# A three-block transformer kernel: mLSTM cells that keep scores and values for a chunk's second visit, with gate rows spread by DMA, and an output projection by seven products

## The chip, the cores and the metric

The kernel is one program on one core of a Trainium2 chip. The metric is the device time of one execution, in microseconds. All data are float32.

## What is computed

Three transformer blocks run one after the other on a sequence of 1024 tokens with 1024 channels. The change touches two places.

In the first block a bidirectional mLSTM runs over the sequence, with 4 heads (key width 64, value width 128), in chunks of 128 tokens, once forward and once backward over the same q, k and v, with gates of their own:

```python
def step(carry, blk):                      # one chunk of one direction
    C, n, m = carry
    b = jnp.cumsum(fb, axis=-1)
    D = jnp.where(lower, b[..., :, None] - b[..., None, :] + ib[..., None, :], -jnp.inf)
    m_t = jnp.maximum(b + m[..., None], D.max(-1))
    s = jnp.einsum('bhtd,bhsd->bhts', qb, kb) * jnp.exp(D - m_t[..., None])
    num = jnp.einsum('bhts,bhsv->bhtv', s, vb) + w_inter[..., None] * jnp.einsum('bhtd,bhdv->bhtv', qb, C)
    h = num / jnp.maximum(jnp.abs(den), jnp.exp(-m_t))[..., None]
    C_new = decay[..., None, None] * C + jnp.einsum('bhs,bhsd,bhsv->bhdv', wk, kb, vb)
```

Its normalised sum of both directions, beside a Fourier mixing of the other channels, is multiplied with `w_out` (named mix in the kernel), and `x = LN(ALPHA * x + (1 + g1) * mix)` follows. The second block holds latent attention (8 heads over 1024 tokens, causal) whose result is multiplied with a 1024 x 1024 matrix and added:

```python
o = causal_block_attention(q, k, v).reshape(B, S, ATTN_WIDTH)
x = x + (o * jax.nn.silu(gate)) @ w_out     # mla_out in the kernel
h = rmsnorm(x, conv_norm_g)
```

## The kernel before

The kernel is written in Bass: the program of each engine is written out by hand, and each cross-engine dependency is a wait on a semaphore. `steps(tag, names)` makes one semaphore with a list of names; `did(name)` raises it and `after(0, name)` is the wait for it. Each engine works strictly in the order in which its program is written. Activations lie with channels on the 128 partitions: X, H and the three parts A, B, C of one tensor ABC hold 8 tiles of 128x1024 each. Weights stream from HBM through a ring of 4 slots, in tiles of 128x1024, issued on SyncE's queue (SP). PSUM is one tensor, bank, of 8 banks of 128x512.

**The cells.** A cell is one chunk of one direction. There are 16; cell n is direction n % 2 and chunk n // 2 counted from that direction's start, so that cells 0 to 7 meet all eight chunks for the first time and cells 8 to 15 meet each for the second time. TensorE's order is front(n+1), back(n). Its front: four matmuls that copy a gate row of each head onto all 128 partitions by a selection matrix (L1187, into bank 0), two more for the weights of the queries (L1192, bank 1), four transposes of the values (L1197), four scores (L1203), two transposes of the keys (L1208). Its back: `out` of cell n, four matmuls with the weighted scores (L1220) and four with the running state (L1224), then `state` (L1231), whose result goes to bank 6. VectorE (DVE), for cell n+1: adds the causal mask to the copied rows (L1696, into weights_t), scales the queries (L1698), copies the values out of PSUM (L1703), multiplies scores and weights (`probs`, L1707); then for cell n: four operations on four columns, of which L1717 is the first and the reciprocal L1723 the last, and two that update the state (L1726). ScalarE (ACT), for cell n+1: four exponentials of the masked rows (`weights`, L1404), four scalings of the keys (L1408); then four that write out cell n (L1415) with the reciprocals. Behind cells 12, 14 and 15 DVE also takes statistics of finished chunks, whose two directions GpSimd (POOL) has added (L978). The first matmul behind the cells is L1253.

During the cells POOL multiplies the reloaded x by ALPHA (L980). The reload, one DMA of 4 MB (L964), is issued before the position transform that stands ahead of the cells. VectorE's first wait for it stands ahead of L313, the first of the small operations that prepare the fused layer norms.

**mla_out.** TensorE multiplies tile by tile (`linear`, L184): 8 output tiles by 2 halves of the tokens by 8 products of 128x128 by 128x512; each such product is two MATMUL instructions in the trace. VectorE adds each bank to X (L2485), ScalarE squares it and VectorE sums the squares for the norm that follows (L578). Other large projections of the kernel (`Seven`, `seven_products`, L718) already compute a pair of output tiles by seven block products in place of eight, from sums of the weights made by POOL (`seven_lhs`, L705 to L713, s1 to s4) and sums of the right-hand side (t1 to t4).

## Time and profile before

| | |
|---|---|
| median of 3 runs | 4214.31 us (4209.85 to 4216.12) |
| the profiled execution's own time | 4215.86 us |
| its span | 4214.1 us |
| TensorE busy | 4126.5 us, 98% of the span |
| VectorE, ScalarE, GpSimd busy | 1640.6, 823.3 and 787.9 us |
| the chain that ended last | TensorE 91%, VectorE 4%, ScalarE, issue, DMA and GpSimd 1% each |
| granted TensorE clock | 0.992 on the mean |

The span is the time from the first to the last instruction; the profiled execution's own time lies 1.8 us above it. A busy time counts an engine as busy while an instruction of its is in flight, whether the engine goes at its full rate or not.

### The profile page before, as it was taken

Reading aid. Unit: us, or ns where it says so; the run is one execution under the profiler, and the core shown is the slowest. Engines: PE = TensorE matmul, PEld = TensorE weight load, DVE = VectorE, ACT = ScalarE, POOL = GpSimd, SP = SyncE. Lnnn points to the kernel's source line nnn. Section 1 sums busy time; section 2 is a strip of 40 time slices with the busy share of each in tenths; the row PEclk is TensorE's granted clock in tenths of the full one; section 3 lists DMA queues with packets and bytes.
Section 4 is the critical chain, followed back from the end, with each engine's and each line's share of the span. In section 5 each row is a group of like instructions: output and inputs, shape, how many; then the busy total and the mean of one; then the engine's idle time right before and its main releaser. Section 6 shows DMA issues by size and latency. Waiting matters only on the chain.

```text
span 4214.1 us, 46243 instructions
## 1 busy us (share of the span) xinstructions
PE 4126.5 (98%) x19608; PEld 2128.0 (50%) x19608; DVE 1640.6 (39%) x2754; ACT 823.3 (20%) x1612; POOL 787.9 (19%) x511
## 2 busy tenths in 40 slices
PE   8999999999999999999999999999999999999999
PEld 3466444444444456664444444654599344444444
DVE  3656263333333323331799431535433322222311
ACT  3124110000002113221332311633243100000000
POOL 3320052324230200000363200000100032212210
PEclk9999999999999999999999999999999999999999
DMA  5420011111111120000111121001100121111121
GB/s 203 169 79 11 30 41 49 40 50 40 40 50 46 75 80 18 28 16 30 40 40 40 40 80 50 31 28 46 61 4 24 40 80 50 40 41 50 61 94 34
DMA packets 53629, 218.50 MB, mean 52 GB/s; under 512 B 6192, under 2 KB 7728, under 8 KB 51504
## 3 DMA queue, kind: packets, MB, share of 16 engines
q1 hardware_dynamic: 47520, 167.53, 11.5%
q0 software_dynamic: 5904, 48.01, 3.0%
q8 instruction: 156, 2.56, 0.2%
q14 instruction: 49, 0.40, 0.0%
HBM read 194.50 MB, written 18.89 MB: 51 GB/s over the span
## 4 chain that ended last, share of the span: by engine, by line
PE 91%; DVE 4%; ACT 1%; issue 1%; DMA 1%; POOL 1%; SPq 0%; DVEq 0%; POOLq 0%; ACTq 0%
PE bank L718 34%; PE bank L184 27%; PE bank L3227 4%; PE bank L3045 4%; PE bank L2054 2%; PE bank L3238 2%; PE bank L2143 1%; PE bank L2113 1%; PE bank L501 1%; PE bank L2929 1%; PE bank L2913 1%; PE bank L2097 1%; PE bank L2134 1%; PE bank L2944 1%; PE bank L3168 1%
## 5 line engine op out<-in xcount | busy, mean ns | idle before, releaser
L184 PE MATMUL bank<-H,ring 128*128 128x512 f32 x1792 | 778.1, 595 | 6.7 <-DVE ABC L3558 2.9
L184 PEld LDWEIGHTS bank<-H,ring 128*128 128x128 f32 x1792 | 339.5, 191 | 435.2 <-issue 430.6
L184 PE MATMUL bank<-ABC,ring 128*128 128x512 f32 x944 | 412.0, 594 | 1.1 <-DVE ABC L1836 0.7
L718 PE MATMUL bank<-H,ring 128*128 128x512 f32 x736 | 323.6, 592 | 1.0 <-ACT ABC L2221 0.8
L184 PEld LDWEIGHTS bank<-ABC,ring 128*128 128x128 f32 x944 | 177.2, 190 | 225.6 <-issue 222.8
L2522 DVE SCALAR_TENSOR_TENSOR bank<-ABC,params,bank 128x1024 f32<-128x1024 f32 x184 | 237.3, 1290 | 8.0
L718 PEld LDWEIGHTS bank<-H,ring 128*128 128x128 f32 x736 | 139.6, 190 | 178.0 <-issue 178.0
L718 PE MATMUL bank<-X 128*128 128x512 f32 x400 | 181.6, 597 | 3.1 <-POOL X L708 3.1
L3045 PE MATMUL bank<-H 64*64 64x64 f32 x5088 | 169.3, 220 | 10.7 <-DVE H L3662 6.0
L718 PE MATMUL bank<-H,X 128*128 128x512 f32 x400 | 179.8, 592 | 0.0
L3045 PEld LDWEIGHTS bank<-H 64*64 64x64 f32 x5088 | 160.0, 136 | 15.7 <-issue 6.5
L718 PE MATMUL bank<-X,ring 128*128 128x512 f32 x368 | 165.4, 592 | 0.0
L718 PE MATMUL bank<-ABC,ring 128*128 128x512 f32 x360 | 157.6, 592 | 0.0
L2000 POOL TENSOR_TENSOR ABC<-ABC 128x1024 f32<-128x1024 f32 x48 | 113.3, 2361 | 220.4 <-ACT ABC L2311 214.7
L1466 ACT ACTIVATE norm_room<-bank 128x512 f32<-128x512 f32 x30 | 17.9, 597 | 637.9 <-PE bank L718 637.9
L718 PEld LDWEIGHTS bank<-X 128*128 128x128 f32 x400 | 76.5, 191 | 100.0 <-issue 100.0
L718 PEld LDWEIGHTS bank<-H,X 128*128 128x128 f32 x400 | 76.0, 190 | 95.9 <-issue 95.2
L705 POOL TENSOR_TENSOR X<-ring 128x512 f32<-128x512 f32 x32 | 41.3, 1290 | 393.7 <-DMA ring<-in_gu 185.1
L718 PEld LDWEIGHTS bank<-X,ring 128*128 128x128 f32 x368 | 69.9, 190 | 88.0 <-issue 87.9
L718 PEld LDWEIGHTS bank<-ABC,ring 128*128 128x128 f32 x360 | 68.4, 190 | 86.1 <-issue 85.1
L718 PE MATMUL bank<-ABC,kept 128*128 128x512 f32 x256 | 111.2, 592 | 0.0
L1828 DVE SCALAR_TENSOR_TENSOR ABC<-bank,params,norm_room 128x512 f32<-128x512 f32 x60 | 45.0, 750 | 153.0 <-PE bank L718 153.0
(686 smaller groups left out, 5866.4 us busy)
## 6 DMA issues: line engine op xcount, KB each, us to landing
ABC<-in_ada SPq DMA_DIRECT2D x48, 512.0 KB, 5.1
ring<-in_gu SPq DMA_DIRECT2D x44, 512.0 KB, 4.4
ring<-in_up SPq DMA_DIRECT2D x32, 512.0 KB, 4.1
...
```

The lines of the kernel that those rows point to most:

```text
L184: mm = nc.tensor.matmul(bank[:, 2 * (m % 2) + h, :], ring[:, s % RING, k * P:(k + 1) * P], rhs(k)[:, h * HALF:(h + 1) * HALF], start=(k == ...
L501: mm = nc.tensor.matmul(bank[:, 2 * m + j, :], ring[:, s % RING, k * P:(k + 1) * P], half_of(H, k, j), start=(k == 0), stop=(k == DT - 1), ...
L718: mm = nc.tensor.matmul(S.bank(j, slot), lhs[:, k * P:(k + 1) * P], rhs[:, k, :], start=start and k == 0, stop=(k == 3), skip_group_check= ...
L1828: nc.vector.scalar_tensor_tensor(dst, product, par("b_ff1", 8 * g + tile_), base, ALU.add, ALU.add).then_inc(*S.did(f"c{c}", j))
L2000: nc.gpsimd.tensor_tensor(C[:, c, :], C[:, c, :], conv_parts[k % 2], ALU.add).then_inc(*conv_pool.did(f"tap{k}"))
L2054: mm = nc.tensor.matmul(bank[:, b + h, :], tile_of(hd, first + k), A[:, src + k, h * HALF:(h + 1) * HALF], start=(k == 0), stop=(k == n - 1))
L2097: return nc.tensor.matmul(score_bank(n)[:, a:z], own_half[side, LENGTHS[n] * P:(LENGTHS[n] + 1) * P], k_pe[side, a:z], start=False, stop=T ...
L2113: nc.tensor.matmul(score_bank(m)[:, a:z], q_n[:, b * P:(b + 1) * P], k_n[:, a:z], start=True, stop=False, skip_group_check=True)
L2522: nc.vector.scalar_tensor_tensor(conv_rows(c), conv_us[c % 4][:, k:k + SEQ], conv_tap(c, k), conv_rows(c), ALU.mult, ALU.add).then_inc(*co ...
L3045: mm = nc.tensor.matmul(bank[rows, b, q * width:(q + 1) * width], lhs(q)[rows], rhs(q)[rows], start=start and (q == 0 or stop), stop=stop, ...
L3227: mm = nc.tensor.matmul(bank[:, down_bank[b], :], lhs[:, k * P:(k + 1) * P], rhs[:, k, :], start=start and k == 0, stop=stop and k == 7, s ...
L3238: mm = nc.tensor.matmul(bank[:, down_bank[b], :], ring[:, down_tile(j, m, part) % RING, k * P:(k + 1) * P], half_of(ABC, 11 * part + k, h) ...
```

## The change

In the cells the copied rows come by DMA. SyncE writes the two kinds of gate rows to HBM (`rows_kept`) and reads them back for each cell, spread over the partitions, into three buffers in turn; the read for cell n waits for `out` of cell n-3. POOL adds the causal mask. Scores and values of a chunk are copied to X in its first visit and used again in its second. In the second visit the keys are scaled by one VectorE operation. The state product goes to banks 0 and 6 in turn, and the reciprocals have two buffers. The unscaled x is reloaded behind the cells, and ALPHA is put into the gain `mod[:, 16:24]` and into the layer norm's epsilon. In the second block, output tiles 0 to 5 of mla_out are made in three pairs by seven products each, and tiles 6 and 7 as before. Two of the seven products of the first pair stand in the last attention head's order. The sums of squares go by a room in SBUF.

```diff
-                dst = bank[:, N.banks[0] + h, :]
+                dst = bank[:, N.banks[0] + h, :] if N.room is None else N.room[:, h, :]
...
-            weights_t = [carve(512) for _ in range(2)]
+            weights_t = [carve(512) for _ in range(3)]
...
+            values = [by_head(X_flat[:, 516 * c:516 * c + 516]) for c in range(7)] + [carve(516, "p (h v) -> p h v", h=4)]
+            scores_kept = [X_flat[:, 4 * SEQ + 512 * c:4 * SEQ + 512 * c + 512] for c in range(NT)]
+            queries = [carve(256, "p (q t) -> p q t", q=2) for _ in range(3)]
...
# SyncE
+            stream(sp, "mix", 0, 2)
+            sp.wait_ge(*rows_dve.after(0, "r"))
+            sp.wait_ge(*rows_act.after(0, "r_wi"))
...
+            for n in range(CELLS):
+                i, d, c, now = cell_of(n)
+                if n == 3:
+                    stream(sp, "mix", 2, 4)
+                if n >= 3:
+                    sp.wait_ge(*cell_pe.after(0, f"out{n - 3}"))
+                sp.dma_start(weights_t[n % 3], rows_kept[0, d, c].rearrange("h t -> (h t)").partition_broadcast(P)
+                             ).then_inc(rows_spread[n % 3], 16)
+                for e in range(2):
+                    sp.dma_start(queries[n % 3][64 * e:64 * e + 64], rows_kept[1, d, c, 2 * e:2 * e + 2, :].partition_broadcast(64)
+                                 ).then_inc(rows_spread[n % 3], 16)
...
# GpSimd
-            pool.dma_start(X[:, :, :], io["x"]).then_inc(x_again, 16)
...
+            def masked(n):
+                i, d, c, now = cell_of(n)
+                pool.wait_ge(*spread_of(n))
+                rows = weights_t[n % 3].rearrange("p (h t) -> p h t", h=4)
+                nc.gpsimd.tensor_tensor(rows, rows, causal[:, d:d + 1, :].broadcast_to([P, 4, P]), ALU.add
+                                        ).then_inc(*cells_pool.did(f"masked{n}"))
...
-            for m in range(DT):
-                last = nc.gpsimd.tensor_scalar(X[:, m, :], X[:, m, :], ALPHA_1, None, ALU.mult)
+            for n in range(CELLS):
+                masked(n)
+                if n == 13:
+                    head_sums_of(5)
+            head_sums_of(6)
             pool.wait_ge(*cell_pe.all())
             pool.wait_ge(*cell_dve.all())
+            pool.dma_start(X[:, :, :], io["x"]).then_inc(x_again, 16)
...
# VectorE, for cell m = n + 1
-                    v.wait_ge(*cell_pe.after(0, f"bcast{m}"))
-                    nc.vector.tensor_tensor(weights_t[m % 2] ..., bank[:, 0, :] ..., causal ..., ALU.add)
+                    v.wait_ge(*spread_of(m))
+                    nc.vector.tensor_tensor(queries[m % 3], A[:, 0:2, now], queries[m % 3], ALU.mult
+                                            ).then_inc(*cell_dve.did(f"queries{m}"))
+                    if met_first(m):
+                        v.wait_ge(*cell_pe.after(0, f"values{m}"))
+                        nc.vector.tensor_copy(values[c][:, :, 0:P], by_head(bank[:, 7, :])).then_inc(*cell_dve.did(f"values{m}"))
+                        v.wait_ge(*cell_pe.after(0, f"scores{m}"))
+                        nc.vector.tensor_copy(by_side(scores_kept[c]), bank[:, 2:4, 0:256] ...).then_inc(*cell_dve.did(f"scored{m}"))
+                        v.wait_ge(*cell_dve.after(0, f"scored{m}"))
+                    else:
+                        v.wait_ge(*cell_pe.after(0, f"keys{m}"))
+                        nc.vector.tensor_tensor(keys_tok[m % 2], bank[:, 1, 256:512] ...,
+                                                token_cols[:, 1, c, 32 * d:32 * d + 4].unsqueeze(2).broadcast_to([P, 4, 64]), ALU.mult
+                                                ).then_inc(*cell_dve.did(f"keys{m}"))
+                    v.wait_ge(*cell_act.after(0, f"weights{m}"))
...
+                    nc.vector.tensor_tensor(probs_t[m % 2], scores_kept[c], weights_t[m % 3], ALU.mult).then_inc(*cell_dve.did(f"probs{m}"))
...
# second block, GpSimd: operands of mla_out's seven products
+            nc.gpsimd.tensor_tensor(t1_out, quarter(B, 0, 1), quarter(B, 0, 0), ALU.subtract).then_inc(*rhs_out.did("t1"))
+            seven_lhs(pool, S, 0, "s1", "s2", "s3", "s4")
+            pool.wait_ge(*mla_dve.after(0, "gated7_6"))
+            nc.gpsimd.tensor_tensor(t3_out[:, 0:3], quarter(B, 1, 1)[:, 0:3], quarter(B, 0, 1)[:, 0:3], ALU.subtract
...
+            pool.wait_ge(*mla_pe.after(0, "s7_7"))
...
# second block, TensorE
-            pe.wait_ge(*mla_dve.all())
-            pe.wait_ge(*taken("mla_heads"))
-            linear(pe, "mla_out", lambda k: B[:, k, :],
+            out_rest()
+            out_free = lambda i, slot: seven_out.after(i, {3: "w", 4: "t21", 7: "t22"}[slot])
+            for j in (1, 2):
+                seven_products(pe, seven_out, j, out_rhs, out_free)
+            pe.wait_ge(*seven_out.after(2, "v"))
+            linear(pe, "mla_out", lambda k: B[:, k, :], 6,
```

TensorE in the cells, before: one whole turn, the front of a cell and the back of the one ahead of it. The row numbers are lines of the kernel, and a matmul counts here as one row entry however many instructions the trace shows for it.

```order
L1187 MATMUL bank<-ABC,kept 128x128 x4
L1192 MATMUL bank<-ABC,kept 128x128 x2
L1197 MATMUL bank<-ident,ABC 128x128 x4
L1203 MATMUL bank<-ABC 128x128 x4
L1208 MATMUL bank<-ident,ABC 128x128 x2
L1220 MATMUL bank<-ABC,norm_room 128x129 x4
L1224 MATMUL bank<-ABC 128x129 x4
L1231 MATMUL bank<-ABC 64x129 x4
```

The change, the last turn whose front is a first visit and the first whose front is a second visit: L1236 are the values, L1242 the scores, L1248 the keys, L1260 and L1264 `out`, L1269 `state`.

```order
L1236 MATMUL bank<-ident,ABC 128x128 x4
L1242 MATMUL bank<-ABC 128x128 x4
L1248 MATMUL bank<-ident,ABC 128x128 x2
L1260 MATMUL bank<-X,norm_room 128x129 x4
L1264 MATMUL bank<-ABC 128x129 x4
L1269 MATMUL bank<-X,ABC 64x129 x4
L1248 MATMUL bank<-ident,ABC 128x128 x2
L1260 MATMUL bank<-X,norm_room 128x129 x4
L1264 MATMUL bank<-ABC 128x129 x4
L1269 MATMUL bank<-X,ABC 64x129 x4
```

The two selection lines are gone from every turn, and values and scores from the turns of the second visits.

GpSimd around the cells, before: the reload of x, the constants, the zeroing, the scaling of x, the six sums of finished chunks.

```order
L964 DMA X<-in_x 128x8192
L966 DMA kept<-in_lstm_const 128x1792
L971 MEMSET ABC 128x516 x2
L972 MEMSET ABC 128x516
L980 TENSOR_SCALAR X<-X 128x1024 x8
L978 TENSOR_TENSOR H<-H 128x512 x6
```

GpSimd at the same place in the change: L1019 is the mask, L1025 the sums.

```order
L1005 DMA kept<-in_lstm_const 128x768
L1010 MEMSET X 128x4 x7
L1010 MEMSET ABC 128x4
L1011 MEMSET ABC 128x516
L1019 TENSOR_TENSOR ABC<-ABC,kept 128x512 x14
L1025 TENSOR_TENSOR H<-H 128x512 x2
L1019 TENSOR_TENSOR ABC<-ABC,kept 128x512 x2
L1025 TENSOR_TENSOR H<-H 128x512 x2
L1033 DMA X<-in_x 128x8192
L1025 TENSOR_TENSOR H<-H 128x512 x2
```

The reload of x has moved from ahead of the cells to behind them, and sixteen mask operations stand where the scaling stood.

TensorE from the end of the last attention head through mla_out, in the change: L2210 is the head's output product, L2218 the transpose of it, L2226 the products of the first pair, L720 those of the other two pairs, L184 tiles 6 and 7.

```order
L2226 MATMUL bank<-ABC,ring 128x512 x2
L2218 MATMUL bank<-ident,H 128x128
L2226 MATMUL bank<-ABC 128x512 x2
L2218 MATMUL bank<-ident,H 128x128
L2226 MATMUL bank<-ABC 128x512 x2
L2226 MATMUL bank<-ABC,ring 128x512 x4
L2226 MATMUL bank<-ABC 128x512 x12
L720 MATMUL bank<-ABC,ring 128x512 x12
L720 MATMUL bank<-ABC 128x512 x16
L184 MATMUL bank<-ABC,ring 128x512 x20
L591 MATMUL bank<-mean_of,norm_room 128x1 x4
L184 MATMUL bank<-ABC,ring 128x512 x6
```

Before, one row stood between the last transposes (L2151) and the norm's sums (L589): 116 matmuls of L184, with 12 more behind. Now the pairs take 84 and tiles 6 and 7 take 32.

## Rows read from the trace of the kernel before

**Rows 1.** The page, first part: busy time, share, instructions of TensorE.

```profile
PE 4126.5 (98%) x19608; PEld 2128.0 (50%) x19608; DVE 1640.6 (39%) x2754; ACT 823.3 (20%) x1612; POOL 787.9 (19%) x511
```

**Rows 2.** Timeline of one turn: start, duration, engine, line, operation, [idle before <-releaser].

```profile
320.57 1.16 PE L1187 MATMUL bank<-ABC,kept 64*128 64x128 f32 x8
320.68 0.18 DVE L1723 RECIPROCAL small<-small 128x4 f32<-128x4 f32 x1
320.78 0.58 DVE L1726 SCALAR_TENSOR_TENSOR ABC<-ABC,small,bank 128x129 f32<-128x129 f32 x2
320.89 1.14 ACT L1415 ACTIVATE H<-bank,small 128x128 f32<-128x128 f32 x4 [1.14 <-DVE small L1723]
...
322.10 0.66 PE L1197 MATMUL bank<-ident,ABC 128*128 128x128 f32 x4
322.21 0.69 DVE L1696 TENSOR_TENSOR ABC<-bank,kept 128x512 f32<-128x512 f32 x1 [0.85 <-PE bank L1192]
...
322.82 0.41 DVE L1698 TENSOR_TENSOR ABC<-ABC,bank 128x256 f32<-128x256 f32 x1
322.94 1.28 ACT L1404 ACTIVATE ABC<-ABC,cols 128x128 f32<-128x128 f32 x4 [0.90 <-DVE ABC L1696]
323.14 0.68 DVE L1703 COPY ABC<-bank 128x512 f32<-128x512 f32 x1
...
323.33 0.44 PE L1208 MATMUL bank<-ident,ABC 128*128 128x128 f32 x2
...
323.61 1.06 PE L1220 MATMUL bank<-ABC,norm_room 128*128 128x129 f32 x8
324.12 0.89 ACT L1408 ACTIVATE ABC<-bank,cols 128x64 f32<-128x64 f32 x4
324.32 0.69 DVE L1707 TENSOR_TENSOR norm_room<-bank,ABC 128x512 f32<-128x512 f32 x1 [0.49 <-ACT ABC L1404]
...
325.24 0.66 PE L1231 MATMUL bank<-ABC 128*64 128x129 f32 x8
325.36 0.16 DVE L1717 TENSOR_SCALAR small<-bank 128x4 f32<-128x4 f32 x1 [0.35 <-PE bank L1224]
...
325.95 0.18 DVE L1723 RECIPROCAL small<-small 128x4 f32<-128x4 f32 x1
```

**Rows 3.** Timeline of TensorE: both ends of the cells, and two groups early in them.

```profile
286.55 1.13 PE L1187 MATMUL bank<-ABC,kept 64*128 64x128 f32 x8 [1.94 <-DVE ABC L1666]
...
290.94 2.07 PE L1187 MATMUL bank<-ABC,kept 64*128 64x128 f32 x8
...
296.47 1.87 PE L1220 MATMUL bank<-ABC,norm_room 128*128 128x129 f32 x8
...
378.63 7.13 PE L1253 MATMUL bank<-ABC,ring 128*128 128x512 f32 x16
```

**Rows 4.** Windows: stretch, length, busy by engine, then granted clock, DMA share, GB/s.

```profile
260.00:263.00 3.00, 3.00 (x19) 3.00 (x18) 0.00 (x0) 0.00 (x0) 0.00 (x0) 0.60 0.97 407
293.00:300.00 7.00, 7.00 (x47) 5.75 (x46) 3.25 (x10) 2.37 (x9) 0.00 (x0) 0.63 0.01 2
364.00:368.00 4.00, 2.51 (x24) 2.03 (x23) 3.38 (x17) 1.49 (x6) 0.00 (x0) 1.00 0.00 0
```

**Rows 5.** DMA issues by tile: queue, count, KB each, median us to landing.

```profile
H<-ABC POOLq DMA_DIRECT2D x8, 256.0 KB, 3.2
...
X<-in_x POOLq DMA_DIRECT2D x1, 4096.0 KB, 14.5
```

**Rows 6.** One line of POOL: duration ns min/median/max, first and last start.

```profile
L713 POOL TENSOR_TENSOR X<-ring,X x32: 1257/1272/2256, 78.7 to 3896.3; 128x512 f32<-128x512 f32 x32
```

**Rows 7.** Timeline: DVE's first instruction behind its wait for x.

```profile
407.66 0.16 DVE L313 COPY kept<-params 128x8 f32<-128x8 f32 x1
```

**Rows 8.** Timeline of TensorE: the last transpose of the last head, and mla_out.

```profile
1894.51 0.30 PE L2151 MATMUL bank<-ident,H 128*128 128x128 f32 x1 [0.47 <-DVE ABC L2455]
1895.19 99.83 PE L184 MATMUL bank<-ABC,ring 128*128 128x512 f32 x232 [0.38 <-DVE ABC L2455]
```

318 lines of the change are left out of this document (216 added, 102 removed).

## The prediction

> **What bounds the kernel now.** I read the page first: TensorE is busy for 98% of the span [rows 1], so a change gains what it takes out of TensorE's order, as long as no other engine becomes the bound where TensorE is relieved. The change sits in two stretches: the cells, from 286.55 us to 378.63 us [rows 3], 92.1 us for sixteen cells, and mla_out, which starts at 1895.19 us [rows 8]. For the cells I then read the timeline of one turn [rows 2]. The reader is to see two things in it. TensorE has no gap: L1187, L1197, L1208, L1220 and L1231 begin as the group ahead of them ends. And beside TensorE runs a ring of ACT and DVE that is nearly as long. From one reciprocal to the next it is 5.27 us (320.68 to 325.95): 0.21 until ACT starts to write the cell out (L1415, 1.14), 0.91 in which ACT waits for the masked rows, 1.38 from the start of the exponentials (L1404) to the start of `probs` (L1707), 0.69 of `probs`, 0.35 of waiting for TensorE's `out`, 0.59 from L1717 to the reciprocal. The sum is 5.27.
>
> **The cells, step by step.** TensorE loses the selections in every turn: 320.57 to 322.10, 1.53 us. In the second visits it also loses values and scores, 322.10 to 323.33, 1.23 us. Its turn is then 5.27 - 1.53 = 3.74 us, and 2.51 us in second visits.
>
> The ring decides in their place. POOL now masks far ahead of ACT, so the 0.91 goes; `out` of a cell no longer stands behind the selections, so the 0.35 goes. What is left is 0.21 + 1.14 + 1.38 + 0.69 + 0.59 = **4.01 us**, since the kernel still has ACT write out cell n before it exponentiates for cell n+2, and DVE do `probs` before the reciprocals. `probs` reads SBUF alone now; L1707 with one PSUM operand is the nearest row, and I keep its 0.69. I check the others against 4.01. DVE in a first visit: 0.41 + 0.68 (values) + 0.68 (scores out, taken as a copy like L1703) + 0.69 + 3 x 0.16 + 0.18 + 0.58 = 3.70; in a second visit the two copies go and a scaling of 256 columns comes, 0.41 like L1698: 2.75. ACT: 1.14 + 1.28 + 0.89 = 3.31, and 2.42. A second ring runs through TensorE, because banks 4 and 5 are single: ACT's end of `out` (0.21 + 1.14), then 1.63 of L1220 and L1224 (323.61 to 325.24), then 0.59, with two hand-overs of 0.1: 3.8. All lie under 4.01, but none far under it in the first visits. So moving the keys to DVE in the second visits gives nothing by itself: ACT had the time.
>
> The new feed. The read for cell n waits for `out` of cell n-3, which ends some 0.8 before that cell's reciprocal. The exponentials of cell n start 1.35 after the reciprocal of cell n-2, that is 4.01 + 1.35 = 5.36 after that of cell n-3. Between stand three DMAs (256 + 64 + 64 KB) and a mask. The trace has no such read. Its nearest row is H<-ABC, 256 KB in 3.2 us [rows 5]; by bytes, 384 KB are 4.8, and one after the other at most twice the row, 6.4. I take 4.0, near the single row, because the three are issued together. The mask is 1.27 by POOL's 128x512 rows, 2.26 at the longest [rows 6]. Ready at -0.8 + 4.0 + 1.27 = 4.5, with 0.9 to spare; with 4.8 nothing is lost; with 6.4 and 1.27 the period becomes 5.5, with 6.4 and 2.26 it becomes 6.5.
>
> By the Trainium skill's page GPSIMD Engine Reference (Specifications), GpSimd shares its SBUF interfaces with VectorE and contends with VectorE instructions that have two SBUF inputs; the queries and `probs` become such instructions here. By that rule each mask would cost the long value of [rows 6], still inside the 0.9 us within 0.1; an estimate from that page therefore moves the sum by under 2 us.
>
> How many turns gain. `out` of cells 0 to 14 is followed by a turn with a front. Two of these turns lie in the cold start, treated below; one (cell 12) also has statistics on DVE, which stay. That leaves 12 plain turns and the one with statistics, each shorter by 5.27 - 4.01 = 1.26: 13 x 1.26 = **16.4 us**. The tail (out14, out15, whose ACT wait remains) is unchanged.
>
> The cold start. TensorE had waited 1.94 before the first cell, and soon after it goes at the lower of its two levels, 1.2 of 2.4 GHz: L1187 takes 2.07 at 290.94 where it takes 1.16 later [rows 2, 3], and 293 to 300 has a mean of 0.63 [rows 4], which puts the rise at about 298. At 2.07 / 1.16 = 1.8 cell 1's selections take 2.7, those of cells 0 and 2 some 1.5 each, 6 us that fall away, but what moves up into their place then runs cold itself. I take 4; ends 2 and 6.
>
> Behind the cells. The reload now starts after the last state update, on the old time axis about a microsecond behind 378.63 [rows 3], and takes 14.5 [rows 5]; DVE first asks for x at 407.66 [rows 7]. The 28 us of head norms, gating and first products hide it with 13 to spare; without that cover it would cost up to 14.5. The scaling by ALPHA on POOL had been hidden too and gives nothing. SP's writes of the gate rows (ten small DMAs) stand ahead of the position transform, and the first three cells' reads beside it. The mix tiles 2 and 3 are queued behind the first three cells' reads, tiles 4 on behind the sixteenth's; the first is wanted only when tiles 0 and 1 are done, so both are covered.
>
> Cells: 16.4 + 4 = 20.4 us.
>
> **mla_out.** Three pairs save four 128x512 products each, 12 in all, 24 instructions. 232 instructions take 99.83 us [rows 8], 0.430 each: 24 x 0.430 = **10.3 us**. Two products move into the tail of the last head and fill its waits for DVE, 0.47 and 0.38 [rows 8]: 0.85. The new operands: POOL's three operations of 1536 columns, some 3.8 each by three times [rows 6], start during the last head, the second of them with the head's last scores, and the first product that needs them has three products of 4 x 2 x 0.430 = 3.4 in front of it, two in the head and one behind. DVE's load per pair is about thirteen 512-column operations of 0.69, 9 us in 24. Nothing of this is late. Sum 11.2 us.
>
> **Sum.** 20.4 + 11.2 = 31.6 us; I take off 1.3 for masks at the long value. 30.3 against the profiled execution's 4215.86 (span 4214.1 and 1.8 around it) is 4185.6; the runs' median is 1.55 lower, so **4184 us**.
>
> **Rivals.**
> *The clock falls in the second visits.* TensorE works there for 2.5 of 4.0 us. For it: the clock fell to 0.60 while TensorE looked fully busy with narrow matmuls in 260 to 263 us [rows 4], and it fell as the cells began. Against it: in 364 to 368, with 2.51 of 4.00 us busy, it stayed at 1.00. At the lower level L1220 takes 1.87 and not 1.06 [rows 3]; the ring through TensorE becomes 0.21 + 1.14 + 3.0 + 0.2 + 0.59 = 5.1. Eight such cells at 1.1 more: +9, **4193**; half of them, 4189. The Trainium skill's page TensorE: Matmul & The Clock Gate (A second HAM failure mode: psum-queue depth-cycling) states that small idle gaps between groups of matmuls, when banks are cycled, make the clock swing between its two levels; by that page this rival would happen.
>
> *The spread rows come late.* If the feed takes 4.8 with long masks or 5.5 or so, the period is 4.5 to 5.5: at 5.0, 13 x 1.0 = +13, **4197**. For it: the cells' own chain has 0.9 us of slack and nothing else. Against: the DMA engines' share in the cells is 0.00 to 0.01 [rows 4].
>
> *The seven products bring nothing*, because operands or the extra additions on DVE hold TensorE: +11, **4195**. Other projections of this kernel run so with TensorE at 98%.
>
> *Slower than before.* One mechanism: the feed's round trip becomes the period. It has to exceed 6.5 us per cell (13 x 2.5 = 32.5 us given back), that is, over 6.4 for the three DMAs with every mask at 2.26. At 7.5 us per cell the time is 4184 + 13 x 3.5 = **4230**. Nothing in the rows shows such a read in a quiet stretch.
>
> **How the numbers follow.** Forecast 0.64 (own range 4177 to 4190; 4177 if the cold start gives 6, the ring's hand-overs overlap by 0.1 to 0.2 per engine and masks are short), clock 0.13, late rows 0.13, no gain in mla_out 0.06, slower 0.02, not as any of these 0.02. The range 4176 to 4197 holds the first three and most of the fourth. What a measurement can tell from no change is about 0.2%, 8.4 us, so faster means under 4206: 0.95; same 0.02; slower 0.03.
>
> **What would show each step.** TensorE's `out` (L1260) should come every 4.0 us in the middle of the cells, with ACT back to back from L1415's successor to the exponentials, and idle time of TensorE waiting for ACT or DVE. POOL's mask should end before ACT asks. If ACT's exponentials wait for POOL and POOL for DMA, the late rows are right; if matmul durations double behind cell 8, the clock. The cells should take about 72 us, mla_out to its norm's last sum about 11 us less. The wait for x behind the cells should not appear. I would be wrong above all if a ring that I did not trace holds the first visits, where DVE, TensorE and the ring lie within 0.3 us of each other.

## The result, and the profile after

| | before | after |
|---|---|---|
| median | 4212.08 us (4207.58 to 4216.12, 4 runs) | 4185.34 us (4183.71 to 4190.48, 4 runs) |
| ratio, with its 95% interval | | 0.9939 [0.9922, 0.9956] |
| the profiled execution's own time, span | 4215.86, 4214.1 us | 4184.5, 4181.1 us |
| TensorE busy | 4126.5 us | 4080.3 us |
| granted TensorE clock, mean | 0.992 | 0.993 |

The change makes the kernel 26.7 us faster by the medians. The forecast was 4184 us, 30.3 us under the execution that was profiled before.

The page of the changed kernel, first part, answers to [rows 1]: TensorE has 312 instructions fewer and is busy for 46 us less.

```profile
PE 4080.3 (98%) x19296; PEld 2090.1 (50%) x19296; DVE 1657.8 (40%) x2767; ACT 817.1 (20%) x1583; POOL 817.8 (20%) x541
```

The total hides a miss. I followed the landmarks of TensorE from stretch to stretch:

| from, to | before | after | gain |
|---|---|---|---|
| start of the program, first matmul of the cells | 286.55 | 284.57 | 2.0 |
| the cells, to the first matmul behind them | 92.08 | 76.12 | 16.0 |
| the first matmul behind the cells, to the first of L184 | 36.14 | 36.59 | -0.4 |
| last query-key product of the last head, to the sums of mla_out's norm | 109.11 | 96.84 | 12.3 |
| the whole span | 4214.1 | 4181.1 | 33.0 |

The row behind the cells comes up again with e1. The rest, some 3.2 us, lies in code that the change doesn't touch. The 2.0 ahead of the cells is scatter too: with the new code the first matmul of the cells starts anywhere from 284.4 to 287.0 us in the runs below. The largest pieces are places where the clock was granted differently in the two executions. These windows show two of them (columns as in [rows 4]): before, and then after.

```profile
20.00:60.00 40.00, 36.63 (x191) 20.03 (x184) 22.93 (x46) 19.28 (x28) 0.00 (x0) 0.91 0.58 229
1418.00:1438.00 20.00, 20.00 (x72) 11.90 (x71) 0.81 (x5) 3.53 (x7) 4.98 (x4) 0.83 0.16 53
```

```profile
20.00:60.00 40.00, 36.63 (x196) 19.43 (x189) 22.86 (x46) 20.60 (x29) 0.52 (x1) 0.96 0.59 231
1400.00:1420.00 20.00, 20.00 (x87) 12.28 (x86) 2.42 (x7) 3.53 (x7) 4.96 (x4) 0.91 0.15 53
```

So the two stretches of the change are worth 16.0 + 12.3 = 28.3 us, against 20.4 + 11.2 forecast (31.6, less 1.3). The cells fell short by 4.4 and mla_out brought 1.1 more.

**Where the cells fell short.** I cut them in three by the starts of `out` (L1260): from the cells' first matmul to out of cell 1 it was 16.0 us before and 8.31 after; from out 1 to out 12, eleven turns, 57.90 and 50.00; from out 12 to the first matmul behind, 18.18 and 17.81. The middle piece should have shrunk to 11 x 4.01 = 44.1. This is one of its turns in the timeline of the changed kernel, a first visit (weight loads are left out); it answers to [rows 2].

```profile
308.27 0.69 DVE L1753 TENSOR_TENSOR norm_room<-X,ABC 128x512 f32<-128x512 f32 x1 [0.39 <-DVE X L1742]
308.38 1.70 POOL L1019 TENSOR_TENSOR ABC<-ABC,kept 128x512 f32<-128x512 f32 x1 [2.97 <-DMA ABC<-rows_kept]
...
308.94 0.33 SPq L974 DMA_DIRECT2D ABC<-rows_kept  x1
308.95 0.16 DVE L1763 TENSOR_SCALAR ABC<-bank 128x4 f32<-128x4 f32 x1
309.14 0.97 DVE L1765 TENSOR_TENSOR ABC<-ABC,cols 128x4 f32<-128x4 f32 x1
...
310.14 0.16 DVE L1767 TENSOR_TENSOR ABC<-bank,ABC 128x4 f32<-128x4 f32 x1
310.34 0.18 DVE L1769 RECIPROCAL ABC<-ABC 128x4 f32<-128x4 f32 x1
310.43 0.58 DVE L1772 SCALAR_TENSOR_TENSOR ABC<-ABC,small,bank 128x129 f32<-128x129 f32 x2
310.55 1.14 ACT L1455 ACTIVATE H<-bank,ABC 128x128 f32<-128x128 f32 x4 [1.55 <-DVE ABC L1769]
...
310.93 0.42 DVE L1736 TENSOR_TENSOR ABC<-ABC 128x256 f32<-128x256 f32 x1
...
311.79 1.13 PE L1260 MATMUL bank<-X,norm_room 128*128 128x129 f32 x8 [0.69 <-DVE ABC L1736]
```

Look at L1765. It works on 128x4 numbers, as L1767 does in 0.16 us, and takes 0.97. It starts 0.76 after POOL's mask (308.38) and ends with it (310.08, 310.11). The reciprocal, ACT's `out` and TensorE's next `out` stand behind it. Without the 0.81 the turn of 4.67 us would be 3.86.

The second visits of the same trace (TensorE and the operations beside the mask) show both what was forecast and a second loss.

```profile
321.12 1.13 PE L1260 MATMUL bank<-X,norm_room 128*128 128x129 f32 x8 [1.93 <-DVE ABC L1747]
322.17 1.27 POOL L1019 TENSOR_TENSOR ABC<-ABC,kept 128x512 f32<-128x512 f32 x1 [2.75 <-DMA ABC<-rows_kept]
...
322.21 1.78 DVE L1753 TENSOR_TENSOR norm_room<-X,ABC 128x512 f32<-128x512 f32 x1 [1.20 <-ACT ABC L1443]
...
325.94 2.06 PE L1260 MATMUL bank<-X,norm_room 128*128 128x129 f32 x8 [0.86 <-DVE ABC L1747]
...
331.25 1.13 PE L1260 MATMUL bank<-X,norm_room 128*128 128x129 f32 x8 [1.13 <-DVE ABC L1747]
...
335.11 1.13 PE L1260 MATMUL bank<-X,norm_room 128*128 128x129 f32 x8 [1.13 <-DVE ABC L1736]
```

At 322.21 `probs` (0.69) takes 1.78, again to the end of a mask. At 325.94 `out` takes 2.06 in place of 1.13: the clock has fallen. From 331.25 on the turn is 3.86 us. The windows of the changed kernel around the fall:

```profile
317.00:321.00 4.00, 2.19 (x24) 1.53 (x22) 3.51 (x10) 2.44 (x11) 1.64 (x1) 1.00 0.33 79
321.00:325.00 4.00, 3.88 (x26) 2.90 (x26) 2.70 (x8) 1.48 (x7) 1.27 (x1) 0.66 0.18 49
325.00:329.00 4.00, 3.14 (x17) 2.73 (x16) 1.52 (x4) 1.99 (x8) 1.27 (x1) 0.50 0.41 76
329.00:333.00 4.00, 2.87 (x30) 2.16 (x28) 2.49 (x9) 2.29 (x8) 0.00 (x0) 0.99 0.28 98
```

TensorE had been busy for 2.19 of 4 us before it fell to the lower level, while DVE was held.

**mla_out.** TensorE's timeline at the end of the last head in the changed kernel, which answers to [rows 8]: products of the first pair (L2226) stand where TensorE had waited for DVE, and no wait of TensorE for another engine is left.

```profile
1874.20 0.27 PE L2218 MATMUL bank<-ident,H 128*128 128x128 f32 x1
...
1875.20 1.88 PE L2226 MATMUL bank<-ABC,ring 128*128 128x512 f32 x4
1876.92 0.27 PE L2218 MATMUL bank<-ident,H 128*128 128x128 f32 x1
1877.03 1.88 PE L2226 MATMUL bank<-ABC 128*128 128x512 f32 x4
1878.75 0.27 PE L2218 MATMUL bank<-ident,H 128*128 128x128 f32 x1
1878.86 1.88 PE L2226 MATMUL bank<-ABC 128*128 128x512 f32 x4
1880.58 3.60 PE L2226 MATMUL bank<-ABC,ring 128*128 128x512 f32 x8
```

The wait for x behind the cells doesn't appear: DVE's L313 starts at 390.16, the reload was issued at 362.1 and took 12.4.

### The profile page after: what moved, and what is told of

Its sections match the earlier page's. It is cut to its first block, busy times and chain, and to the rows that moved or that the text cites. A ratio compares the mean times of both kernels' runs of the same rounds, so it can differ in the third digit from the quotient of the medians.

```text
span 4181.1 us, 45680 instructions
## 1 busy us (share of the span) xinstructions
PE 4080.3 (98%) x19296; PEld 2090.1 (50%) x19296; DVE 1657.8 (40%) x2767; ACT 817.1 (20%) x1583; POOL 817.8 (20%) x541
## 4 chain that ended last, share of the span: by engine, by line
PE 84%; DVE 5%; ACT 1%; issue 1%; DMA 1%; POOL 1%; SPq 0%; DVEq 0%; POOLq 0%; ACTq 0%
PE bank L720 32%; PE bank L184 25%; PE bank L3397 4%; PE bank L3215 4%; PE bank L2121 2%; PE bank L3408 2%; PE bank L2210 1%; PE bank L2180 1%; PE bank L501 1%; PE bank L2164 1%; PE bank L3099 1%; PE bank L3083 1%; PE bank L2201 1%; PE bank L3114 1%; PE bank L3338 1%
## 5 line engine op out<-in xcount | busy, mean ns | idle before, releaser
L184 PE MATMUL bank<-H,ring 128*128 128x512 f32 x1792 | 780.5, 596 | 6.2 <-DVE ABC L3728 2.9
L184 PEld LDWEIGHTS bank<-H,ring 128*128 128x128 f32 x1792 | 340.4, 191 | 436.3 <-issue 431.8
L184 PE MATMUL bank<-ABC,ring 128*128 128x512 f32 x752 | 329.5, 595 | 0.7 <-DVE ABC L1882 0.7
L720 PE MATMUL bank<-H,ring 128*128 128x512 f32 x736 | 323.6, 592 | 1.2 <-ACT ABC L2346 0.8
L184 PEld LDWEIGHTS bank<-ABC,ring 128*128 128x128 f32 x752 | 140.8, 190 | 179.6 <-issue 177.3
L720 PEld LDWEIGHTS bank<-H,ring 128*128 128x128 f32 x736 | 139.6, 190 | 178.2 <-issue 178.2
L720 PE MATMUL bank<-X 128*128 128x512 f32 x400 | 179.9, 592 | 3.1 <-POOL X L710 3.1
L720 PE MATMUL bank<-ABC,ring 128*128 128x512 f32 x416 | 182.1, 592 | 0.0
L720 PE MATMUL bank<-H,X 128*128 128x512 f32 x400 | 179.9, 592 | 1.2 <-POOL H L1051 1.2
L720 PE MATMUL bank<-X,ring 128*128 128x512 f32 x368 | 165.5, 592 | 0.0
L720 PEld LDWEIGHTS bank<-ABC,ring 128*128 128x128 f32 x416 | 79.0, 190 | 99.5 <-issue 98.5
L720 PEld LDWEIGHTS bank<-X 128*128 128x128 f32 x400 | 75.9, 190 | 99.1 <-issue 98.9
L720 PEld LDWEIGHTS bank<-H,X 128*128 128x128 f32 x400 | 75.9, 190 | 97.2 <-issue 94.7
L720 PEld LDWEIGHTS bank<-X,ring 128*128 128x128 f32 x368 | 69.8, 190 | 88.2 <-issue 88.2
L720 PE MATMUL bank<-ABC,kept 128*128 128x512 f32 x256 | 111.2, 592 | 0.0
```

Of the source, the lines that this page charges most:

```text
L184: mm = nc.tensor.matmul(bank[:, 2 * (m % 2) + h, :], ring[:, s % RING, k * P:(k + 1) * P], rhs(k)[:, h * HALF:(h + 1) * HALF], start=(k == ...
L720: mm = nc.tensor.matmul(S.bank(j, slot), lhs[:, k * P:(k + 1) * P], rhs[:, k, :], start=start and k == 0, stop=(k == 3), skip_group_check= ...
```

## The experiments

My theory, H: POOL's mask and a VectorE operation that reads two SBUF inputs keep each other waiting, and the feed's timing puts the mask onto L1765. The rivals: VectorE is simply full in the first visits, or L1765 is slow for another reason. All the stretches are in one table behind the experiments. The runs of one kernel lie 4 to 13 us apart, so the stretches carry the argument. A turn is the time from one `out` (L1260) to the next.

**e1 and e2: the two halves apart.** e1 has only the changes to the cells, e2 only those to mla_out. Seen from the changed kernel, e1 has mla_out as it was,

```diff
-            out_rest()
...
+            linear(pe, "mla_out", lambda k: B[:, k, :],
```

and e2, seen from the changed kernel, has among others

```diff
-                    v.wait_ge(*spread_of(m))
...
+                    v.wait_ge(*cell_pe.after(0, f"bcast{m}"))
```

> The kernel before with the change to the cells alone; mla_out is made as before. If the two parts add up, the cells bring here what the profile of the whole change shows for them: 92.1 us before, 76.1 after, from the first matmul of the cells to the first behind them, so 16 us, and the time is about 4212 - 16 = 4196. My blind sum had 19 to 20 for them (4192). Rival: the new cells also disturb or help something behind them (the reload of x, the mix tiles queued behind the reads); then the landmarks behind the cells stand more or less than 16 us earlier than before.

> The kernel before with mla_out by seven products alone. If the two parts add up: 12.3 us of gain, the time about 4200. My blind sum had 11.2. Rival: the sum of the two gains in e1 and e2 differs from the 27 to 28 us of the whole by more than 3 us, so one part helps the other.

e1: 4203.36 us (4196.95 to 4209.77, 10 runs), ratio 0.9981 [0.9972, 0.9991]. e2: 4202.78 (4198.27 to 4209.16, 10 runs), ratio 0.9975 [0.9966, 0.9984]. e2's stretch of mla_out takes 96.83 us, as in the whole change. e1's cells take 78.9 us, 2.8 more than the same code in the whole change, with first visits of 4.67 again. By their times the parts give 0.0044 of the time together and the whole gives 0.0061; with the intervals that is no difference I can tell, though e1 alone gives less by its time (3.8 to 11.8 us) than the 13.2 of its stretch.

The rival of e1 is partly true. From the first matmul behind the cells to the first of L184 it takes 38.2 us, 2.1 more than before, so that the gain of 13.2 has shrunk to 11.1 there: ACT lets TensorE wait 0.94 in place of 0.55, and the clock is at its lower level once more (0.50 over 374 to 377 us; 1.00 over 379 to 400 before), where sixteen of the products take 8.70 in place of 7.03. Seven executions have such a stretch, of 38.2 to 38.4 us (e1, e3, e5, e6, e7, e8, e10); the changed kernel, e4, e9, e11 and e12 have 36.5 to 36.6, and e2 with the old cells 36.2. What decides it wasn't tried.

So mla_out's part is sharp, and that of the cells is 13 to 16 us, depending on how often the mask meets DVE and on how long the clock is low behind cell 12 (0.50 over all of 350 to 363 in e1), less 0.4 to 2.1 behind them.

**e3: the mask made short.** One column of each head is masked, in the same place with the same waits; the exponentials are those of unmasked rows.

```diff
-                nc.gpsimd.tensor_tensor(rows, rows, causal[:, d:d + 1, :].broadcast_to([P, 4, P]), ALU.add
+                nc.gpsimd.tensor_tensor(rows[:, :, 0:1], rows[:, :, 0:1], causal[:, d:d + 1, 0:1].broadcast_to([P, 4, 1]), ALU.add
```

> The changed kernel with the causal mask added to one column of each head in place of 128, so that POOL's operation keeps its place and its waits but is short. The exponentials are then those of unmasked rows: part of the computation is left out. Theory H (a VectorE operation with two SBUF inputs and POOL's mask hold each other up): the 128x4 operation L1765 goes back from 0.97 us to 0.16 in the first visits, their period from 4.67 us to 3.86, and over six or seven turns the cells get 5 to 6 us shorter, 76.1 to about 70.5; time about 4180. Rival R1 (VectorE's own work, or the ring of ACT and DVE, holds the first visits at 4.67, and the long L1765 only fills a wait): the period stays at 4.6 to 4.7 and the cells at 76 us. Rival R2 (the long L1765 is something else, a late semaphore or the read by DMA in flight at that time): L1765 stays at 0.9 or more, since the reads stand as before.

4177.07 us (4172.29 to 4182.05, 4 runs), ratio 0.9921 [0.9906, 0.9936]. The timeline of a first visit in e3:

```profile
305.82 0.69 DVE L1753 TENSOR_TENSOR norm_room<-X,ABC 128x512 f32<-128x512 f32 x1 [0.39 <-DVE X L1742]
...
306.50 0.16 DVE L1763 TENSOR_SCALAR ABC<-bank 128x4 f32<-128x4 f32 x1
306.70 0.16 DVE L1765 TENSOR_TENSOR ABC<-ABC,cols 128x4 f32<-128x4 f32 x1
306.72 0.21 POOL L1019 TENSOR_TENSOR ABC<-ABC,kept 128x4 f32<-128x4 f32 x1 [3.65 <-DMA ABC<-rows_kept]
306.90 0.16 DVE L1767 TENSOR_TENSOR ABC<-bank,ABC 128x4 f32<-128x4 f32 x1
```

L1765 takes 0.16, the turns from out 1 to out 12 are 3.87 us each, first visits and second visits alike, and the cells take 68.9 us. From 289 to 345 us the clock stays at 1.00, though TensorE is busy for only 2.87 of 4 us in the second visits: the fall at 321 us came with the hold. H stands; that VectorE is full (R1) and that the reads slow it (R2) fall, since both are unchanged here.

**e4: the keys back on ACT.** The change's own edit, undone alone.

```diff
-                    if met_first(n + 1):
-                        act.wait_ge(*cell_pe.after(0, f"keys{n + 1}"))
+                    act.wait_ge(*cell_pe.after(0, f"keys{n + 1}"))
...
-                    else:
-                        v.wait_ge(*cell_pe.after(0, f"keys{m}"))
-                        nc.vector.tensor_tensor(keys_tok[m % 2], ...
```

> The changed kernel with the keys of the second visits scaled by ACT in four operations, as in the first visits and as before the change. Theory (the second visits run at the length of a ring, recip, ACT's out, exponentials, probs, and ACT had time for the keys): the period of the undisturbed second visits stays at 3.86 to 3.9, the cells at 76 us within 1, and the time is the same within what can be measured. Rival (VectorE's one operation relieves ACT, as the edit's form suggests): the period grows by up to ACT's 0.93 us, the cells by up to 8 x 0.9 = 7 us. Second rival (the one operation hurts VectorE and TensorE waits for it, as the releaser L1747 in the list of waits says): the period falls by 0.3 to 0.4, the cells by 2 to 3 us.

4186.74 us (4183.29 to 4191.24, 4 runs), ratio 0.9945 [0.993, 0.9959]: the same by its time. But the turns of the second visits were 4.56 to 5.31 us, and out 1 to out 12 took 52.8 us against 50.0 to 51.1 for the code of the change. This looked like the first rival. The timeline of e4 speaks for another reason:

```profile
334.79 0.16 DVE L1757 TENSOR_SCALAR ABC<-bank 128x4 f32<-128x4 f32 x1
334.94 1.26 POOL L1019 TENSOR_TENSOR ABC<-ABC,kept 128x512 f32<-128x512 f32 x1 [3.73 <-DMA ABC<-rows_kept]
334.99 1.24 DVE L1759 TENSOR_TENSOR ABC<-ABC,cols 128x4 f32<-128x4 f32 x1
```

The mask meets the 128x4 operation in the second visits too. Whether ACT's four operations cost anything besides had to be asked without the hold (e9).

**e5: the mask moved in time.** Nothing is left out; POOL waits for VectorE's queries, and a fourth buffer keeps the mask early enough for ACT.

```diff
-            weights_t = [carve(512) for _ in range(3)]
+            weights_t = [carve(512) for _ in range(4)]
...
                 pool.wait_ge(*spread_of(n))
+                if n:
+                    pool.wait_ge(*cell_dve.after(0, f"queries{n - 1}"))
```

> The changed kernel with four buffers for the spread rows in place of three, so that each read is issued one cell earlier, and POOL's mask for cell n waits also for VectorE's queries of cell n-1. Nothing is left out. The mask then starts behind the queries, while VectorE copies from PSUM, in place of beside L1765. Theory H (two engines on two SBUF inputs each hold each other up): L1765 takes 0.16 us in every cell, all plain turns come every 3.87 us as in e3, the cells take 69 to 71 us, the time is about 4178. In the second visits the mask can still touch the start of probs, for 0.1 us. Rival R2 (what e3 removed was the work of the mask as such, or the waits around it): the first visits stay at 4.6 or more. Rival R3 (the hold moves to another operation of VectorE): L1736 or L1753 grow by as much as L1765 shrinks.

4177.16 us (4172.65 to 4184.33, 4 runs), ratio 0.991 [0.9895, 0.9925]. A first visit of e5: the mask stands beside the copies from PSUM.

```profile
311.19 0.42 DVE L1738 TENSOR_TENSOR ABC<-ABC 128x256 f32<-128x256 f32 x1
311.53 0.68 DVE L1742 COPY X<-bank 128x512 f32<-128x512 f32 x1
...
311.75 1.27 POOL L1021 TENSOR_TENSOR ABC<-ABC,kept 128x512 f32<-128x512 f32 x1 [2.58 <-DVE ABC L1738]
...
312.13 0.68 DVE L1744 COPY X<-bank 128x512 f32<-128x512 f32 x1
```

All eleven turns are 3.87 us, 42.53 together, and the cells take 68.85 us. The full mask is made, so it isn't its work but its place that cost 7.3 us beside the changed kernel's 76.12, and 10 beside e1. The fourth buffer isn't what brings it: e3 has the same turns with three.

**e6: TensorE kept busy in the second visits.**

```diff
+                if not met_first(n):
+                    for h in range(4):
+                        nc.tensor.transpose(bank[:, 7, h * P:(h + 1) * P], A[:, 4 + h, now], ident[:, :])
```

> The changed kernel with four transposes per second visit put back in TensorE's order (the values of the chunk once more, into bank 7, read by nobody), 0.66 us each time. The clock had fallen to 0.66 and 0.59 at the first two second visits (321 to 330 us), behind a stretch in which TensorE was busy for 2.19 of 4 us. If the fall is from TensorE's idleness at that place, the two turns of 4.82 and 5.31 us become 3.9 to 4.7, the cells 2 to 3 us shorter. Rival (the fall comes from something else, or from the waits on VectorE, which stay): both turns stay, and the cells are as long as before or up to 0.66 longer per turn where TensorE is the bound. In e3, where the hold was gone, TensorE was busy for 2.87 of 4 us and the clock stayed at 1.00, which speaks for the first.

4190.88 us (4187.2 to 4193.73, 4 runs), ratio 0.994 [0.9923, 0.9956]. My expectation failed: the second visits took 4.83 to 5.07 us, out 1 to out 12 52.9, L1770 (L1765 of the change) had a median of 0.63 us over its 16 cells, and the clock fell to 0.68 at 329 to 333 all the same. The added transposes shifted the second visits so that the mask kept meeting VectorE. So it says nothing about the clock by itself, and no run here fills the place with matmuls other than transposes.

**e7: late rows, made to happen.** Two buffers in place of three.

```diff
-                if n >= 3:
-                    sp.wait_ge(*cell_pe.after(0, f"out{n - 3}"))
+                if n >= 2:
+                    sp.wait_ge(*cell_pe.after(0, f"out{n - 2}"))
```

> The changed kernel with two buffers for the spread rows in place of three: the read for cell n waits for out of cell n-2. This makes the rival of the prediction, late rows, happen. By the rows of the changed kernel the loop over two cells is: issue 0.1, landing 3.9, mask 1.27, exponentials to the start of probs 1.49, probs 0.69, out 0.1 + 1.79, together 9.3 us, 4.67 per cell. The first visits stay near 4.67 (if the mask still meets L1765 there they get longer, up to 5.1), the second visits grow from 3.87 to about 4.67, ACT's exponentials wait for POOL, and the cells take 79 to 84 us, the time 4188 to 4194. If the feed had more slack than I think (a read faster than 3.9 in this pattern), nothing changes.

4212.65 us (4208.61 to 4220.42, 10 runs), ratio 0.9994 [0.9985, 1.0003]: the whole gain is gone. The cells take 103.6 us and out 1 to out 12 71.3, 6.5 per cell where I had 4.67. The list of waits of e7 in its cells (us in total, times, longest) names the mechanism:

```profile
POOL ABC L1019 <- DMA ABC<-rows_kept: 84.2, 14, 23.0
ACT ABC L1443 <- POOL ABC L1019: 32.6, 14, 4.2
...
DVE ABC L1736 <- DMA ABC<-rows_kept: 18.4, 10, 3.3
```

ACT waits for POOL and POOL for the read, as I expected. My loop lacked what stands between `probs` and `out` in the order of the engines: VectorE meets its wait for the rows of cell m (L1736) before it makes the reciprocals of cell m-1, and TensorE's `out` of cell m needs ACT to have emptied the banks of cell m-1. That adds 0.6 + 0.2 + 1.14 + 0.1 = 2.0 to the 9.3. The clock adds the rest: its mean from 300 to 380 us was 0.70, and one `out` (L1260 and L1264) takes 3.2 at the lower level, not 1.8. That makes 12.7 for two cells, as in the trace, where turns of 7.39 and 5.31 follow each other.

**e8: the first pair's two products behind the head.**

```diff
-                    if not after and g == 7:
-                        out_first(0, 2)
...
+            out_first(0, 4)
+            out_fifth(0, 4)
             out_rest()
```

> The changed kernel with the two products of mla_out's first pair taken out of the last attention head and put ahead of the rest of the pair. The stretch from the last query-key product of the last head to the first matmul of block 3's stretch at 2663 us took 797.0 us in the changed kernel and 810.3 before. By my prediction the two products fill 0.85 us of waits, so 797.9 here; by the trace, in which the tail of the head shrank from 4.29 to 2.42 us beside its own work, 1.87, so 798.9; if their place brings nothing, 797.0. The device time can't tell these apart.

4189.48 us (4183.27 to 4194.89, 4 runs), ratio 0.9937 [0.9922, 0.9952]. The stretch that I had named ends too far behind: it takes 796.8 to 799.7 us in the kernels that share mla_out with the change, and 799.9 here. To the sums of mla_out's norm it is sharp, 96.83 to 96.84 in all eleven with the pair in the head, and 98.23 in e8. So the place in the head is worth 1.4 us, between my 0.85 and the 1.87 that I had read out of the trace.

**e9: e4's edit without the hold** (e5 with the keys of every cell on ACT).

> e5 (four buffers, the mask held back behind the queries) with the keys of the second visits scaled by ACT in four operations. In e4, without the wait for the queries, this edit brought periods of 4.6 to 5.3 in the second visits against 3.87, and L1759 took up to 1.24 us beside a mask. Theory: e4 lost nothing by ACT's four operations, it lost because the mask came to lie beside the 128x4 operation in the second visits too. Then here all plain turns are 3.87 as in e5 and the cells are as long as in e5 (68.9 us) within 1. Rival: VectorE's single operation brings something by itself; then the second visits are 4.2 or longer and the cells 3 us or more longer than in e5.

4177.2 us (4175.78 to 4180.59, 4 runs), ratio 0.9911 [0.9892, 0.993]. All eleven turns are 3.86 to 3.87, 42.51 together. VectorE's one operation in place of ACT's four brings nothing. The cells are 0.9 us longer than in e5, all of it behind cell 12, a piece that scatters: it is 17.8 to 20.1 us in the three executions of the change's own cells.

**e10: filling the tail** (e5 with the transposes of e6 for cells 12 to 15).

> e5 with the chunk's four value transposes put back into TensorE's order for cells 12 to 15 (into bank 7, read by nobody). In e5 the turns behind cell 12, where VectorE also takes statistics, were 4.63, 6.02 and 5.09 us; TensorE was busy for 2.11 and 1.68 of 4 us from 337 to 345, and the clock then fell to 0.64. If TensorE's idleness there is what lets the clock fall, the second and third of these turns become 4.6 to 5.3 and the cells 1 to 2 us shorter than 68.9. Rival: the idle time is one wait for VectorE, which four narrow transposes don't fill; the clock falls all the same and the cells are as long or 0.7 longer. In e6 the same filling in the changed kernel took nothing away, since the hold of VectorE by the mask lengthened its turns by more.

4182.35 us (4179.35 to 4183.25, 4 runs), ratio 0.9919 [0.9903, 0.9935]. The turn of 6.02 stayed at 6.03, the clock fell to 0.55 at 349 to 353, and the piece behind cell 12 took 19.15 us against 18.04. The rival was right, and the cells were even 1.1 us longer than in e5, where it had 0.7. The long turn has a cause of its own, the same hold in a new place, as the timeline of e5 shows:

```profile
342.14 1.26 POOL L1021 TENSOR_TENSOR ABC<-ABC,kept 128x512 f32<-128x512 f32 x1 [2.74 <-DVE ABC L1738]
342.25 1.70 DVE L1755 TENSOR_TENSOR norm_room<-X,ABC 128x512 f32<-128x512 f32 x1
```

**e11: POOL with one input.** Zero is added to the rows; the mask is left out.

```diff
-                nc.gpsimd.tensor_tensor(rows, rows, causal[:, d:d + 1, :].broadcast_to([P, 4, P]), ALU.add
+                nc.gpsimd.tensor_scalar(rows, rows, 0.0, None, ALU.add
```

> The changed kernel with POOL's mask, an addition of two SBUF inputs, replaced by an addition of zero to the rows, one SBUF input of the same 128x512. The mask is left out of the computation. POOL's one-input operations of 128x1024 took 2.76 us in the kernel before, so about 1.4 us here. If VectorE's two-input operations are held by any operation of POOL, L1765 still takes 0.9 to 1.2 us in the first visits, with a period near 4.7, and the cells 74 to 79 us. If only a two-input operation of POOL holds them, L1765 takes 0.16, the period is 3.87 and the cells 69 to 70 us.

4178.76 us (4175.49 to 4183.67, 4 runs), ratio 0.9913 [0.9895, 0.993]. Neither expectation: the operation takes 1.49 us, L1765 takes 0.16 to 0.58 outside the tail, the turns are 3.86 to 4.34. Two places in the timeline of e11:

```profile
309.18 1.49 POOL L1019 TENSOR_SCALAR ABC<-ABC 128x512 f32<-128x512 f32 x1 [2.48 <-DMA ABC<-rows_kept]
...
309.88 0.42 DVE L1736 TENSOR_TENSOR ABC<-ABC 128x256 f32<-128x256 f32 x1
...
312.78 1.49 POOL L1019 TENSOR_SCALAR ABC<-ABC 128x512 f32<-128x512 f32 x1 [2.11 <-DMA ABC<-rows_kept]
312.86 0.54 DVE L1765 TENSOR_TENSOR ABC<-ABC,cols 128x4 f32<-128x4 f32 x1
```

Queries that start 0.70 us into POOL's operation aren't held; L1765, 0.08 into it, is, but only until 0.46 us after POOL's start (312.86 + 0.54 - 0.16 - 312.78).

**e12: the last mask let go** (e5, in which the mask of cell 15 waits for the queries of cell 13).

```diff
-                    pool.wait_ge(*cell_dve.after(0, f"queries{n - 1}"))
+                    pool.wait_ge(*cell_dve.after(0, f"queries{min(n - 1, 13)}"))
```

> e5 with one wait changed: the mask of cell 15 waits for the queries of cell 13 in place of 14, so it follows the mask of cell 14 at once. It tests the rule that the other traces gave, in a place not used to find it: a VectorE operation with two SBUF inputs begins 0.14 us before the end of a two-input operation that POOL has begun, and one with a single SBUF input isn't held. In e5 the mask of cell 15 ran from 342.14 to 343.40 and probs (0.69 us) from 342.25 to 343.95, 1.70. Moved up, the mask lies beside the statistics (one SBUF input, 0.87 and 0.38 us per four), which then keep their length, and probs takes 0.69. The turn of 6.02 us becomes 5.0, or less if the clock does not fall; the cells take 67 to 68 us in place of 68.9, the time 4175 to 4178. Rival: the statistics are held in their place and grow by about 1 us; the cells stay at 68.9. VectorE's 128x4 operation beside the sums of finished chunks stays at 0.9 us, twice, in both cases.

4173.78 us (4172.36 to 4176.47, 4 runs), ratio 0.9902 [0.9885, 0.9918]. In its timeline the two masks lie beside the state update and the statistics, which keep their length, and `probs` is 0.68:

```profile
338.61 2.48 POOL L1021 TENSOR_TENSOR ABC<-ABC,kept 128x512 f32<-128x512 f32 x2
...
339.49 0.86 DVE L1720 BATCH_NORM_STATS2 ABC<-H 128x6 f32<-128x128 f32 x4
...
342.72 0.68 DVE L1755 TENSOR_TENSOR norm_room<-X,ABC 128x512 f32<-128x512 f32 x1
```

The turn fell from 6.02 to 5.10 as expected. The cells as a whole hardly did (68.68 against 68.85). In e5 the clock fell once, to 0.64 at 345 to 349 us; here it fell twice, to 0.62 at 341 to 345 and to 0.59 at 351 to 355. From `out` of cell 15 to the first matmul behind it was 3.51 us here and 2.30 in e5, which took most of the gain back. This kernel has the lowest median of all, but its runs overlap with those of e5.

The stretches of the cells in us, each from one profiled execution, with the median of the runs:

| kernel | first matmul to out 1 | out 1 to out 12 | out 12 to behind | cells | median |
|---|---|---|---|---|---|
| before | 16.00 | 57.90 | 18.18 | 92.08 | 4212.08 |
| after | 8.31 | 50.00 | 17.81 | 76.12 | 4185.34 |
| e1 cells only | 8.29 | 51.08 | 19.55 | 78.92 | 4203.36 |
| e2 mla_out only | 16.01 | 57.90 | 18.18 | 92.09 | 4202.78 |
| e3 short mask | 8.29 | 42.55 | 18.08 | 68.92 | 4177.07 |
| e4 keys on ACT | 8.32 | 52.84 | 17.93 | 79.09 | 4186.74 |
| e5 mask moved | 8.28 | 42.53 | 18.04 | 68.85 | 4177.16 |
| e6 filled | 8.32 | 52.91 | 18.58 | 79.81 | 4190.88 |
| e7 two buffers | 8.32 | 71.29 | 24.00 | 103.61 | 4212.65 |
| e8 (cells as after) | 8.33 | 50.90 | 20.14 | 79.37 | 4189.48 |
| e9 moved, keys on ACT | 8.28 | 42.51 | 19.00 | 69.79 | 4177.20 |
| e10 moved, tail filled | 8.32 | 42.51 | 19.15 | 69.98 | 4182.35 |
| e11 one input | 8.28 | 44.68 | 17.36 | 70.32 | 4178.76 |
| e12 last mask free | 8.28 | 42.54 | 17.86 | 68.68 | 4173.78 |

## Why the prediction was right, and where it was not

**The time was right by errors against each other, and by luck.** The two stretches gave 28.3 us where the sum had 30.3. The turns behind out 1 gave 8.3 where I had 16.4; the cold start gave 7.7 for 4, mla_out 12.3 for 11.2, and 1.3 had been taken off for long masks. In the three executions of the new cells as they are (after, e1, e8) the cells gave 16.0, 13.2 and 12.7, so the changed kernel's own execution was the best of three. And the forecast stood on a median before of 4214.31; with the fourth run it is 4212.08, which makes the miss in the gain, 26.7 for 30.3, larger than that in the time, 1.3.

**The ring.** It was 3.87 us where nothing disturbs it (e3, e5, e9), forecast 4.01. The difference is overlap: ACT's exponentials start 1.02 after its `out` does, not 1.14. Eleven turns by 5.27 - 3.87 are 15.4 us. The step that failed is the mask's: "By that rule each mask would cost the long value of [rows 6], still inside the 0.9 us". I let the contention lengthen only POOL's operation, which had slack, and priced it at under 2 us, 1.3 in the sum. The other side of it, VectorE held on the ring, cost 7.4 us from out 1 to out 12 (50.00 - 42.53): in six first visits 0.75 to 1.08 each, 5.0 together; 0.95 at the first second visit; and 1.44 in the turn behind it, in which the clock was at its lower level. The prediction named the danger only in general, as a ring that it did not trace.

The trace of the kernel before could have shown the other side. Far behind the cells an operation on 128x8 numbers lies beside one of POOL:

```profile
549.99 4.50 POOL L998 TENSOR_TENSOR X<-H 128x2048 f32<-128x2048 f32 x1 [14.61 <-DVE H L432]
550.10 4.42 DVE L1793 SCALAR_TENSOR_TENSOR small<-params,small 128x8 f32<-128x8 f32 x1
```

L1790, on as many numbers and just ahead of them, takes 0.16.

**Behind cell 12.** The 16.4 us hold thirteen turns, and the prediction called the tail behind them unchanged. The two turns from out 12 to out 14 gave 1.9 us of 2.5 (in e3, without the mask, all of it). But from out 14 to the first matmul behind the cells it was 6.09 us before and 7.61 after, 1.5 longer, and 8.45 in e3. TensorE is at its lower level there (0.50 over 353 to 356 us in the changed kernel, 0.50 over 347 to 353 in e3), where it had 1.00 over 364 to 378 before; in e3 `out` of cell 15 takes 2.06 and not 1.13. The clock fell behind cell 12 in every execution of the new cells and in neither of the old ones. So the 8.1 us missing behind out 1 are 6.0 in the eleven turns, 0.6 in the next two and 1.5 in the tail.

**The cold start.** From the first matmul to out 1 it gave 7.7 us in every kernel with the new cells. I had taken 4, with 6 as the end; as a term it was mis-sized. In the windows of the changed kernel the clock is back at 1.00 at 289 us; before, it was 0.63 over 293 to 300 [rows 4]. I had let what moves up run cold as long as before. Why the clock came back sooner isn't shown.

**The rivals.** The clock did fall in the second visits, in the changed kernel, but behind a hold, and it cost 1.4 us where the rival had 9. In e3 and e5, with TensorE busy for 2.87 of 4 us and banks cycled as before, it stayed at 1.00 up to 345 us. By the rule that I had made a rival, of the Trainium skill's page TensorE: Matmul & The Clock Gate (A second HAM failure mode: psum-queue depth-cycling), it would have swung there too. It fell only behind cell 12, where TensorE was busy for 1.68 of 4 us (341 to 345 in e5). The late rows did not come with three buffers: the mask starts 3.9 to 4.3 us after the issue, once 4.6, near the 4.0 that I took, but the slack in the second visits is 0.32 us (a mask ends at 334.57, ACT starts at 334.89) and 0.03 one turn later, not 0.9. The periods of 5.5 and 6.5 for late reads were wrong in themselves: by the prediction's own terms the reciprocals of cell n-3 stand 2.66 us (1.38 + 0.69 + 0.59) behind the exponentials of cell n-2, so what comes late is spread over two cells, and the same reads, ready 6.87 (-0.8 + 6.4 + 1.27) and 7.86 (with 2.26) behind those reciprocals, give (2.66 + 6.87) / 2 = 4.8 and (2.66 + 7.86) / 2 = 5.3. Their price with a buffer fewer was far above mine: 27.5 us in the cells against the 13 of the rival, since a late row also stalls the reciprocals and lets the clock fall.

**The keys.** "By itself nothing" was right (e9). e4 taught that undoing such an edit can change the time of other things: it moved the meeting of two engines.

**mla_out.** The 10.3 for 24 instructions is right. The waits were worth 2.0 us where I had 0.85. I had left out the 0.44 at 1892.80, and the hand-over ahead of the first product, which e8 also fills. The pair in the head is worth 1.4 of it (e8), the rest is that the first product needn't wait for the last transpose.

**What stays open.** Whether a filling with other matmuls than transposes would hold the clock in the tail wasn't tried, nor what makes it fall again behind the cells in some kernels.
